# First chunk step of the attention and state-scan stage: next group's parameter copy ahead of the corner tiles, R copies ahead of the first exponentials

## The reference, cut to what matters

```python
logits = jnp.einsum('bqhmd,bkhmd->bhmqk', q_blk, k).astype(jnp.float32)
logits = logits + bias.transpose(2, 0, 1)[None, :, None]
p = jax.nn.softmax(logits, axis=-1)
attn = p[:, :, 0] - lam * p[:, :, 1]
...
sa = jnp.einsum('bhij,bhj->bhi', state, -kk_t)
state = (state * w_t[:, :, None, :] + sa[..., None] * (kk_t * a_t)[:, :, None, :]
         + v_t[..., None] * k_t[:, :, None, :])
y_t = jnp.einsum('bhij,bhj->bhi', state, r_t)
```

## Time and profile before

| | |
|---|---|
| median of 3 runs | 4278.34 us (4276.24 to 4279.28) |
| the profiled execution, its own time | 4285.27 us |
| its span, first to last instruction | 4283.4 us |
| PE busy | 4141.5 us, 97% |
| DVE busy | 1414.3 us, 33% |
| ACT busy | 868.6 us, 20% |
| mean granted TensorE clock | 0.992 |

### The profile page before, as it was taken

The page is one execution under the profiler, slowest core; times in us unless marked ns, Lnnn a source line. Parts: engine busy times, 40 slices in busy tenths (PEclk is TensorE's granted clock), DMA queues, the critical chain, the costliest instruction groups (busy, mean ns, idle before and its releaser), DMA issues.

```text
span 4283.4 us, 60619 instructions
## 1 busy us (share of the span) xinstructions
PE 4141.5 (97%) x25176; PEld 2695.0 (63%) x25176; DVE 1414.3 (33%) x3578; ACT 868.6 (20%) x2216; POOL 324.8 (8%) x274
## 2 busy tenths in 40 slices
PE   8999999999999999999999999899999999999999
PEld 4666664444444666674434444687887788788878
DVE  4666631121002666650121000432234431323342
ACT  4232320010001233320010000332322212223220
POOL 0122300000000023210000000000110000011000
PEclk9999999999999999999999999999999999999999
DMA  3011112212221111002222222111111121111111
GB/s 121 33 37 35 45 41 88 80 63 79 74 79 64 50 45 45 31 22 94 85 69 72 76 78 74 54 55 55 59 55 53 57 69 60 50 60 60 57 58 64
DMA packets 71487, 261.60 MB, mean 61 GB/s; under 512 B 7936, under 2 KB 8064, under 8 KB 70960
## 3 DMA queue, kind: packets, MB, share of 16 engines
q1 hardware_dynamic: 69312, 250.62, 16.8%
q10 hardware_dynamic: 1904, 7.11, 0.5%
HBM read 253.51 MB, written 4.19 MB: 60 GB/s over the span
## 4 chain that ended last, share of the span: by engine, by line
PE 94%; DVE 3%; issue 1%; ACT 1%; DVEq 1%; ACTq 0%; DMA 0%; SPq 0%
PE ps L2238 30%; PE ps L1422 26%; PE ps L2372 10%; PE ps L2337 4%; PE ps L1441 2%; PE ps L1525 2%; PE ps L815 2%; PE ps L1585 2%; PE ps L773 2%; PE ps L2249 1%; PE ps L1544 1%; PE ps L2259 1%; PE ps L805 1%; PE ps L2280 1%; PE ps L858 1%
## 5 line engine op out<-in xcount | busy, mean ns | idle before, releaser
L2238 PE MATMUL ps<-xT,ring 128*128 128x512 f32 x2656 | 1163.4, 598 | 23.6 <-ACT xT L2428 23.6
L2238 PEld LDWEIGHTS ps<-xT,ring 128*128 128x128 f32 x2656 | 505.8, 192 | 657.9 <-issue 653.8
L1422 PE MATMUL ps<-xT,ring 128*128 128x264 f32 (+2 forms) x3392 | 782.7, 386 | 0.0
L1422 PEld LDWEIGHTS ps<-xT,ring 128*128 128x128 f32 (+1 forms) x3392 | 633.7, 190 | 110.3 <-issue 10.8
L2372 PE MATMUL ps<-arena,ring 128*128 128x512 f32 x1024 | 440.4, 593 | 1.9 <-issue 1.9
L2372 PEld LDWEIGHTS ps<-arena,ring 128*128 128x128 f32 x1024 | 194.5, 190 | 247.9 <-issue 247.9
L1422 PE MATMUL ps<-arena,ring 128*128 128x264 f32 (+1 forms) x1408 | 321.8, 386 | 5.9 <-DVE arena L1902 3.6
L1422 PEld LDWEIGHTS ps<-arena,ring 128*128 128x128 f32 x1408 | 266.7, 191 | 50.9 <-DVE arena L1902 5.1
L1672 ACT ACTIVATE arena<-ps 128x264 f32<-128x264 f32 (+8 forms) x316 | 122.3, 388 | 619.2 <-PE ps L1422 544.0
L2625 DVE TENSOR_TENSOR arena<-arena 128x512 f32<-128x512 f32 x64 | 44.3, 692 | 394.6 <-ACT arena L2491 394.6
L2337 PE MATMUL ps<-yT,ring 128*128 128x512 f32 x384 | 167.6, 593 | 2.3 <-ACT yT L1039 2.3
(11 more groups left out here) (334 smaller groups left out, 4599.8 us busy)
## 6 DMA issues: line engine op xcount, KB each, us to landing
ring<-in_weights SPq DMA_DIRECT2D x467, 512.0 KB, 3.4
arena<-skew_dram ACTq DMA_DIRECT2D x8, 448.0 KB, 3.0
arena<-in_x SPq DMA_DIRECT2D x1, 2048.0 KB, 7.6
out_rows<-arena SPq DMA_DIRECT2D x8, 256.0 KB, 2.9
skew_dram<-arena ACTq DMA_DIRECT2D x4, 511.5 KB, 5.8
consts<-in_const SPq DMA_DIRECT2D x1, 1256.0 KB, 10.2
consts<-in_const ACTq DMA_DIRECT2D x1, 1252.0 KB, 5.5
consts<-in_const SPq DMA_DIRECT2D x1, 128.0 KB, 2.3
```

Of the source, the lines that this page charges most:

```text
L1422: mm = pe.matmul(o[0:m, 0:cols.stop - cols.start], ws[:, k, 0:m], src[:, k, cols], start=k == 0, stop=k == nk - 1)
L2238: m = pe.matmul(o, w[:, k, :], src[:, k, 0:S], start=k == 0, stop=k == KD - 1)
```

## The change

In `group_act` the pair `probs(0)` moves from ahead of the chunk loop to behind the two copies of `R00` and `R10`, in all eight groups (four for each layer). In `group_dve` the call `load_params(c + 1)` moves from behind the four copies of the corner tiles to ahead of them, in groups 0 to 2 of each layer (six calls).

```diff
             take("gate", gate)
-            probs(0)
             for s in range(NCH):
                 for d in range(2):
                     take(f"R{d}{s}", Rs[d], n=P)
+                if s == 0:
+                    probs(0)
                 if s:
...
             rowmax(0)
+            if c < GROUPS - 1:
+                load_params(dve, L, c + 1)
             for d in range(2):
                 for h in range(2):
                     o = v.open(N(f"T{d}{h}_{HB}"))
...
-            if c < GROUPS - 1:
-                load_params(dve, L, c + 1)
             chunk = [list(range(NCH)), list(range(NCH - 1, -1, -1))]
```

## The result

The change made the kernel slower: a median of 4293.81 us (4289.67 to 4297.98, 6 runs) against 4277.70 us (4275.69 to 4280.73, 6 runs), a ratio of 1.0033 [1.0023, 1.0043], that is 14 us, from 10 to 18 (95% interval). The profiled execution took 4291.77 us, its span 4290.0 us. The forecast was 4283.0 us in a range from 4277.5 to 4288.5 us.

A forecast was written before the change was run, and what follows sets the result against it. PE, 94% of the chain of waits, was taken to bound the kernel. The ACT edit's +5.46 and the DVE edit's -0.8 gave +4.7 us, from a median of 4278.34 to 4283.0 us, range 4277.5 to 4288.5.

The forecast's parts named there:

- The ACT edit in groups 3: In both groups 3, exponentials behind the R copies and an exposed table load start S 2.73 us later each, +5.46 us.
- the gain from earlier R copies: In groups 3, copying R00 and R10 earlier gains nothing: PE releases R10, and U follows logits(1).
- The drain: Rival, groups 3: ACT empties ahead of the table load, some 1.4 us more each, up to +3.4, 4286.4 us; chance 0.08.
- The cover in groups 0 to 2: In groups 0 to 2, projection zk on PE hides the exponentials' 1.0 us delay, costing nothing; rival that it fails 0.02.
- The DVE edit: In six groups, PE's parameter wait mostly becomes a wait ahead of logits(1); 0.13 us gained each, -0.8 us.
- The clock falls in the longer pause (slower): Rival, groups 3: clock falls shortly before S, 3.2 us each; both groups 4289.4 us, chance 0.07; one 4286.2, 0.10.

The follow-up runs named there:

- split_groups: The change, but with probs(0) ahead of the R copies again in groups 3; 4277.71 us, ratio 0.9988 to the kernel before.
- only_act: The kernel before with only probs(0) moved behind the R copies, the parameter copy as before; 4293.69 us, ratio 1.0029 to the kernel before.

## Why the prediction was wrong

- **The ACT edit in groups 3: right.** A shift of `S` by 2.73 us was worked out; it was 3.69 - 1.17 = 2.52 in layer 0 and 2.65 in layer 1, 5.2 us in all against 5.46. Most of the rest is the pair of exponentials, put at 1.68 us and here 1.52 (561.86 to 563.38). The load took 1.28 us with the exponential 0.01 us behind its end, and the gain from earlier R copies was nil: `U` still started 3.2 us behind the corner products (558.05 to 561.23, before 556.99 to 560.17).
- **The drain: did not happen.** The row of the load above starts 0.02 us after the copy ends and the exponential follows at once. The 2.66 us of the Trainium skill, ScalarE: Activation LUTs, section What ACT_TABLE_LOAD costs, do not hold here; the measurement decides.
- **The cover in groups 0 to 2: right**, by `split_groups` and the 6.01 us of DVE's idle time that are left.
- **The DVE edit: right in kind, small in size.** 0.13 us for each group were taken; the six gains in the trace are four of 0.24 to 0.28, one of 0.61 and one of -0.05, 1.6 us in all against 0.8. Its own run can't be told from zero.
- **The step that failed is the clock.** The sum put it at nothing. It stood among the rivals, "The clock falls in the longer pause (slower)", with 0.07 for both groups, where six of six fell. Two steps of it were wrong. First its chance: it rested on one pause of 5.91 us, taken for the rule, and on "the other pauses of this trace with a fall were longer too". That sentence was false: the same trace had a fall behind a wait of 1.04 us, in the very stage at issue, and two of 3.4 us near waits of 1.91 and 2.33 us (near 3549.5 and 3651.9). The stage was at the edge already. Second its price: 3.2 us for each group, with 6.8 us at the low clock taken from dense products; in the change it lasted 10.2 us and cost 4.9 us. With both falls at that price the rival came to 4289.4 us, still below the 4293.81 measured.

With these the sum closes: waits +5.2, parameter copy -1.6, clock 2 x 4.9 = +9.7, less what the kernel before loses there by itself (one fall in the four stages of its two traces, 3.25 us, so 1.6 us for each execution; the ten stages with such a wait give 1.6 as well): +11.7 us, inside the measured 10 to 18. The two profiled executions differ by only 6.5 us, since the first trace of before held such a fall and single executions vary by several microseconds elsewhere. Some of that is no matter of the clock: from the corner products of group 0 to those of group 3 in layer 0, at a granted clock of 1.00 throughout, the two traces of before took 387.36 and 390.56 us. What makes up the distance from 11.7 to the middle of 14 was not looked into.

The warning of the Trainium skill, TensorE: Matmul & The Clock Gate, section Why this matters for your kernels, against idle gaps between bursts of matmuls agrees with the change's two falls, behind waits of 3.69 us. But what it says of long gaps is no licence for short ones: `S` waited 1.04 us in the kernel before and the clock fell.

## What to carry to other kernels

Before moving a step on one engine, ask what it would now stand behind: a ready exponential put behind a copy whose data come 1.8 us later also drags its table load out of a pause. A wait in a stage of small products can cost more than its length (here 2.5 us more of waiting cost 7.4); look at the granted clock of that very stage, in more than one trace, before pricing it. And where a step is moved because someone waits for it, look for the one tile that the next in line hangs on: one corner copy first, not none or all four, turned a gain of 1.6 us by the trace into one of 7.7 (8.6 by the ratio).

## What was not expected of the hardware

- In five of the six falls behind a wait of 3.7 us the clock stayed at 1.2 GHz for 10.2 us over small products, with PE busy in every slice (the sixth, layer 1 of `only_act`, 6.8 us). It came back after 6.8 us under dense 128x512 products behind a pause of 5.91 us, and over the same small products behind two of the waits of 1.0 to 1.2 us; behind the third it was 3.4 us. Why it mostly stays down longer behind the long wait was not tried.
- Products of no use in a wait are a cure: 3.65 us of them kept the clock at 1.0 and saved 4.9 us in each group 3, and still lose to removing the wait.
